# Input projection of a hybrid attention layer: each 128-row matmul issued as two 64-row matmuls, one on each half of the array

## What is computed

```
h = rms_norm(x) * norm_pre
p = h @ w_in                       # 2048 -> 7168 columns: q, k, v, gate of heads A (12), B (12 q / 4 kv), C (8)
oa = stick_breaking(qa, ka, va)    # causal over everything before
ob = band_attention(qb, kb, vb, 2 chunks back, alibi, sinks)
oc = band_attention(qc, kc, vc, 8 chunks back, relative bias)
o = concat(oa * silu(ga), ob * silu(gb), oc * silu(gc)) @ w_out
y = x + rms_norm(o) * norm_post    # and the new k, v rows as outputs
```

## Time and profile before

| | |
|---|---|
| median of three executions | 1939.62 us |
| span of the profiled execution, first to last instruction | 1936.8 us |
| PE busy | 1905.3 us, 98% |
| DVE busy | 1240.0 us, 64% |
| ACT busy | 666.4 us, 34% |
| share of PE in the chain that ended last | 86%, of it 61 points products |
| mean granted clock of TensorE | 0.997 |
| DMA | 301 MB, mean 155 GB/s |

### The profile page before, as it was taken

The page is one execution under the profiler, slowest core; times in us unless marked ns, Lnnn a source line. Parts: engine busy times, 40 slices in busy tenths (PEclk is TensorE's granted clock), DMA queues, the critical chain, the costliest instruction groups (busy, mean ns, idle before and its releaser), DMA issues.

```text
span 1936.8 us, 30940 instructions
## 1 busy us (share of the span) xinstructions
PE 1905.3 (98%) x12508; PEld 1746.7 (90%) x12508; DVE 1240.0 (64%) x2224; ACT 666.4 (34%) x1257; POOL 53.3 (3%) x119
## 2 busy tenths in 40 slices
PE   6999999999999999999999999999999999999997
PEld 5999999999999999999999999999999988888886
DVE  7358777787878778553544454355525566766878
ACT  7124233343433334222222222233213354344453
POOL 4000000000000000000000000000000000000131
PEclk9999999999999999999999999999999999999999
DMA  6456777676777767666657667465446657555396
GB/s 245 117 120 137 159 157 165 145 147 154 146 162 154 162 146 149 151 137 136 149 119 155 141 136 143 104 141 123 106 97 144 136 197 278 192 175 187 121 258 226
DMA packets 880407, 301.05 MB, mean 155 GB/s; under 512 B 618504, under 2 KB 845592, under 8 KB 878968
## 3 DMA queue, kind: packets, MB, share of 16 engines
q1 hardware_dynamic: 877192, 290.35, 61.6%
q0 software_dynamic: 3072, 8.73, 2.2%
HBM read 210.45 MB, written 96.20 MB: 158 GB/s over the span
## 4 chain that ended last, share of the span: by engine, by line
PE 86%; DVE 9%; DMA 1%; ACT 1%; issue 1%; POOL 0%; SPq 0%; DVEq 0%; ACTq 0%; POOLq 0%
PE ps L1204 21%; PE ps L1205 20%; PE ps L1206 20%; PE ps L1400 4%; PE ps L1401 4%; PE ps L1402 4%; PE ps L1292 3%; PE ps L1371 3%; PE ps L1264 2%; PE ps L1342 2%; DVE arena L1853 1%; DVE act_lo L1740 1%; DVE arena L1733 1%; DMA b_out<-in_w_out_dram 1%; DVE arena L1841 1%
## 5 line engine op out<-in xcount | busy, mean ns | idle before, releaser
L1204 PE MATMUL ps<-act_hi,w_hi 128*128 128x352 f32 x2688 | 878.8, 327 | 0.1
L1206 PE MATMUL ps<-act_hi,w_lo 128*128 128x352 f32 x2688 | 863.7, 321 | 0.0
L1205 PE MATMUL ps<-act_lo,w_hi 128*128 128x352 f32 x2688 | 863.6, 321 | 0.0
L1204 PEld LDWEIGHTS ps<-act_hi,w_hi 128*128 128x128 f32 x2688 | 505.2, 188 | 24.7 <-issue 20.7
L1205 PEld LDWEIGHTS ps<-act_lo,w_hi 128*128 128x128 f32 x2688 | 506.1, 188 | 0.0
L1206 PEld LDWEIGHTS ps<-act_hi,w_lo 128*128 128x128 f32 x2688 | 504.9, 188 | 0.0
L1501 ACT ACTIVATE w_hi<-w_raw 128x512 fp32r<-128x512 f32 x224 | 139.3, 623 | 340.5 <-DMA w_raw<-in_w_in_dram 340.4
L1748 DVE TENSOR_TENSOR w_lo<-w_raw,w_hi 128x512 fp32r<-128x512 f32 x224 | 150.9, 675 | 51.5 <-ACT w_hi L1501 51.2
L1568 ACT ACTIVATE arena<-arena,small 128x257 f32<-128x257 f32 (+6 forms) x180 | 101.3, 565 | 209.1 <-DVE small L1891 209.1
L2079 DVE STREAM_TRANSPOSE arena<-arena 128x1024 f32<-128x1024 f32 (+4 forms) x100 | 132.6, 1326 | 40.0 <-ACT arena L1691 39.2
L1691 ACT ACTIVATE arena<-arena 128x1024 f32<-128x1024 f32 (+1 forms) x60 | 61.0, 1017 | 255.8 <-DVE arena L1865 255.7
(11 more groups left out here) (182 smaller groups left out, 2105.5 us busy)
## 6 DMA issues: line engine op xcount, KB each, us to landing
w_raw<-in_w_in_dram SPq DMA_DIRECT2D x176, 256.0 KB, 3.3
weight_scratch<-arena SPq DMA_DIRECT2D x216, 128.0 KB, 3.4
arena<-weight_scratch SPq DMA_DIRECT2D x54, 512.0 KB, 4.5
b_out<-in_w_out_dram SPq DMA_DIRECT2D x72, 256.0 KB, 3.3
w_raw<-in_w_out_dram SPq DMA_DIRECT2D x70, 256.0 KB, 2.7
w_raw<-in_w_in_dram SPq DMA_DIRECT2D x96, 128.0 KB, 3.1
weight_scratch<-arena SPq DMA_DIRECT2D x80, 132.0 KB, 4.1
arena<-weight_scratch SPq DMA_DIRECT2D x40, 256.0 KB, 3.3
```

What stands on the lines that cost most here:

```text
L1204: mm(bank(g, GN), wh, ah, start=(k == 0), stop=False)
L1205: mm(bank(g, GN), wh, al, start=False, stop=False)
L1206: last = mm(bank(g, GN), wl, ah, start=False, stop=(k == KT - 1))
```

## The change

Tiles 1 to 55 get another way of being multiplied; tile 0 keeps `product`. Each 128-row matmul becomes two of 64 rows, one on partitions 0 to 63 (`upper`), one on partitions 64 to 127 (`lower`), with the same 128 output partitions and 352 columns. Both add into the same PSUM bank, but not at the same time: in the list of PE an upper matmul number x is followed by the lower matmul number x - 15, which belongs to another group and so to another bank. The first lower matmul of a product waits until its upper twelve are done, the first upper one of the next quarter until the lower twelve are done. A tick now holds 12 upper and 12 lower matmuls, and a product is complete 15 matmuls (1.25 ticks) later than before. For that, all attention is moved back by one tick (`SLOT`), the fetching and splitting of weights too (`piece_at`), and the evacuation of a group by 1.2 ticks. The counts of the semaphore `piece_used` are adapted, since each product now adds to it.

```diff
-SLOT = [12 * (FIRST[u] - 1) for u in range(NU)]
+SLOT = [12 * (FIRST[u] - 1) + 1 for u in range(NU)]
...
+LAG = 15
+def used_no(T, q, g=2):
+    return 9 * T + (3 * g + q if T == 0 else 3 * q + g) + 1
...
 def piece_at(T, q):
-    return 12 * (T - 2) + 3 * q + 3.0
+    return 12 * (T - 2) + 3 * q + 4.0
...
-    plan += [(12 * (T - 1) + 9.9 + g, "out", T, g) for T in range(TILES) for g in range(GROUPS)]
+    plan += [(12 * (T - 1) + 11.1 + g, "out", T, g) for T in range(TILES) for g in range(GROUPS)]
...
-            def project(T, n):
-                q, g = divmod(n, GROUPS)
-                if g == 0:
-                    pe.wait_ge(lo_made, 4 * T + q + 1)
-                if q == 0:
-                    pe.wait_ge(proj_out, 3 * (T - 1) + g + 1)
-                last = product(g, q)
-                if q == 3:
-                    last.then_inc(proj_done, 1)
-                elif g == GROUPS - 1:
-                    last.then_inc(piece_used, 1)
+            def half_product(half, n, x):
+                q, g = divmod(n, GROUPS)
+                kk, part = divmod(x, 3)
+                k, hp = 4 * q + kk, slice(64 * half, 64 * half + 64)
+                w = (w_hi, w_hi, w_lo)[part][hp, q, P * kk:P * kk + P]
+                a = (act_hi, act_lo, act_hi)[part][hp, k, GN * g:GN * g + GN]
+                return mm(bank(g, GN), w, a, start=(half == 0 and k == 0 and part == 0),
+                          stop=(half == 1 and k == KT - 1 and part == 2), skip_group_check=True)
+            def upper(s, x):
+                T, n = s // 12 + 1, s % 12
+                q, g = divmod(n, GROUPS)
+                if x == 0:
+                    if g == 0:
+                        pe.wait_ge(lo_made, 4 * T + q + 1)
+                    if q == 0:
+                        pe.wait_ge(proj_out, 3 * (T - 1) + g + 1)
+                    else:
+                        pe.wait_ge(piece_used, used_no(T, q - 1, g))
+                last = half_product(0, n, x)
+                if x == 11:
+                    last.then_inc(upper_done, 1)
+            def lower(s, x):
+                T, n = s // 12 + 1, s % 12
+                if x == 0:
+                    pe.wait_ge(upper_done, s + 1)
+                last = half_product(1, n, x)
+                if x == 11:
+                    last.then_inc(proj_done if n >= 9 else piece_used, 1)
+            def project(s):
+                for x in range(12 * s, 12 * s + 12):
+                    upper(s, x % 12)
+                    if x >= LAG:
+                        lower((x - LAG) // 12, (x - LAG) % 12)
+                if s + 1 == TICKS:
+                    for x in range(12 * TICKS - LAG, 12 * TICKS):
+                        lower(x // 12, x % 12)
```

More of the change, by code:

```diff
@@ L468, in sp_plan @@
             k, v = 12 * TILE_OF["k", u], 12 * TILE_OF["v", u]
-            plan += [(k + 3.0, "store_keys", u, 0), (v + 0.6, "part_values", u, 0), (v + 8.0, "load_values", u, 0),
+            plan += [(k + 3.0, "store_keys", u, 0), (v + 1.6, "part_values", u, 0), (v + 8.0, "load_values", u, 0),
                      (v + 12.0, "store_values", u, 0), (cache_at(u), "cache_keys", u, 0), (SLOT[u] + (14.5 if 0 < u < NA else 10.5 if u == NA else 6.0), "cache_values", u, 0)]
@@ L768, in build @@
         hi_made, lo_made, piece_used = sem("hi_made"), sem("lo_made"), sem("piece_used")
-        proj_done, proj_out = sem("proj_done"), sem("proj_out")
+        proj_done, proj_out, upper_done = sem("proj_done"), sem("proj_out"), sem("upper_done")
         kc_in, kc_turned, vc_in = sem("kc_in"), sem("kc_turned"), sem("vc_in")
@@ L918, in in_piece @@
                 if T and q < 3:
-                    sp.wait_ge(piece_used, 3 * (T - 1) + q + 1)
+                    sp.wait_ge(piece_used, used_no(T - 1, q))
                 elif T:
@@ L1064, in piece_out @@
                 elif r < 3:
-                    sp.wait_ge(piece_used, 3 * (TILES - 1) + r + 1)
+                    sp.wait_ge(piece_used, used_no(TILES - 1, r))
                 else:
@@ L1085, in mixed_load @@
                 if q < 3:
-                    sp.wait_ge(piece_used, 3 * (TILES - 1) + q + 1)
+                    sp.wait_ge(piece_used, used_no(TILES - 1, q))
                 else:
@@ L1225, in first_project @@
                     last = product(g, q)
[L1226 to L1229, removed]
+                    last.then_inc(proj_done if q == 3 else piece_used, 1)
             def set_ready(key):
@@ L1427, in _ @@
                 if what == "product":
-                    project(u, n)
+                    project(12 * (u - 1) + n)
                 elif what == "scores" and UNITS[u][0] == "a":
@@ L1589, in left_high @@
                 else:
-                    act.wait_ge(piece_used, 3 * (TILES - 1) + (1, 1, 2, 2, 2, 2, 3, 3)[k])
+                    act.wait_ge(piece_used, used_no(TILES - 1, (0, 0, 1, 1, 1, 1, 2, 2)[k]))
                 wait_left_raw(act, i, k)
@@ L1600, in sample_high @@
                     return
-                act.wait_ge(piece_used, 3 * TILES)
+                act.wait_ge(piece_used, 9 * TILES)
                 if n == 2:
```

## The result

The changed kernel takes **1972.47 us** (median of four executions, 1969.58 to 1973.47), the kernel before 1939.25 us in the same job (four, 1938.63 to 1939.85). The ratio is 1.017 with an interval of 1.0157 to 1.0184: 33 us slower, where 65 us faster had been forecast. The profiled execution of the changed kernel took 1972.42 us; its span is 1970.7 us, 33.9 more than before.

A forecast was written before the change was run, and what follows sets the result against it. PE was taken to bound the kernel, busy for 1905 of 1937 us. The terms, -63.4 - 14.0 + 2.3 + 10 = -65.1 us, gave 1874.5 us, with a range of 1846 to 1948.

The forecast's parts named there:

- term 1: Product matmuls: a pair of 64-row halves leaves a 4.3 ns gap beyond streaming instead of 12.3 ns; -63.4 us.
- term 4: Evacuation of product groups from PSUM: PE waits where DVE is late, one wait a tile; +10 us, 16.6 at most.
- Rival (a): Product matmuls: the 12.3 ns gap stays for each half; 1936 us, 1928 without waits, 1945 with all; chance 0.36.
- Term 2: Between scores and products: 70 changes of the array's form, 0.20 us each, are spared; -14.0 us.
- Term 3: Start and end of the products: fifteen upper and fifteen lower halves run without a partner, 15 slots more; +2.3 us.
- At nothing: Weight fetch and split, semaphore waits of lower matmuls, and PE's issue of two loads and two matmuls: no cost.
- Rival (b): Product pairs: float32r weight loads of the halves go one after the other, 212 to 217 ns; some 2370 us; chance 0.14.
- (c): Product pairs: each costs 1 to 3 ns more than a whole matmul, +16 us; about 1952 us; chance 0.08.

## Why the prediction was wrong

Two steps failed: the gap that term 1 took from the scores, which had to bring nearly all of the gain, and the size of the waits in term 4.

- **Term 1** (-63.4 us) failed and gave 0. The step in question was "I take 4.3 ns, a pair every 151 ns, since the scores are the nearest rows in form". The gap is the same for a whole matmul, a pair and a lone half: 159.1 ns each. What makes the scores' gap small is not their 64 rows. The prediction named the row that said so, the float32 passes on all 128 rows with 0.43 to 0.46 us for 0.427, and made it a rival. They are float32 like the scores, with a load for each pass, but stand on all 128 rows (and on 64 output partitions): a small gap does not need the 64 rows. The pass of 0.43 us and a pair at the lower clock both take 0.83 to 0.84 ns a column, and both show next to no gap; whether the type or the pace decides, no run separates. Rival (a), with a chance of 0.36, had the size by symmetry: each half gets what the whole array got.
- **Term 2** (-14.0) was right in the main: 0.20 us at the place shown, -12.6 us between the two kernels with ACT's evacuation, -10.7 in the change itself, where waits lie in the same steps. The page "TensorEngine Tiling (Array Packing)" of the Trainium skill (Key Properties) says that a change of tiling mode drains TensorE; the trace agrees and gives the price, 0.09 us to drain and 0.11 for the load behind.
- **Term 3** (+2.3) was right: the 30 lone halves have the ordinary step, 15 x 0.159 = 2.4.
- **Term 4** (+10, at most 16.6) was too small: 32.9 us. The mechanism was named, and for the v tiles the size was near (11.6 us of idle time), though there the due times are enough and the later product is not needed (9.9 with whole matmuls). The bound was wrong in three ways. It took the evacuations of k tiles to keep their place, though the list of DVE has one a unit behind four scans now; this was half of it (16.0 us). It counted only one wait a tile. And it counted no cost but the idle time, where a wait also costs the overlap with the last pair and uncovers a load. The clock behind waits, 6.4 us, stood in no term.
- **Sum by the same terms with the measured values**: 0 - 10.7 + 31.4 + 5.8 + 4.8 + 2.1 = +33.4. Rival (a)'s highest time, 1945, used the same bound of 16.6 and was 27 us short, so the range, which took (a) as its far end, did not hold. The rows of one v tile gave no bound for what happens at the k tiles.
- **At nothing**: right. The issue of four records in 159 ns holds (halves and whole have the same step), no wait of the products for the splitting stands in PE's view of waits. The queue that loads instructions moved 2.64 MB instead of 1.62, with no stop of PE to be seen for it.
- Rival (b) is refuted by every pair: the loads overlap. So is (c), 159.1 against 159.1.

What stays open: what the gap is, of which a bfloat16 step keeps 8.7 ns; why the clock falls behind some waits of 2 us and not behind others; and one to two us of ordinary steps in the kernels with halves.

## What to carry over

Splitting a full-height matmul into row halves bought no throughput here: the gap is as long for a half, a pair and a whole matmul, and the halves only pay where they spare a change of the array's form, 0.20 us each. A change that lets results come later by a tick must be checked in the list of the engine that takes them out, entry by entry, since two tenths of a tick decided between ahead of and behind a 2.4 us block; a wait there costs 0.28 us more than its idle time, and sometimes the clock. The slack of an idle engine (ACT here, 15.5 us) was worth more than the order on the busy one.

## What the hardware showed beyond this

- A 64-row float32r matmul alone, a pair on the two halves, and a whole one: 159.1 ns a step each for 352 columns at 2.4 GHz. At 1.2 GHz nine steps of pairs take 287.14 - 284.50 = 2.64 us, 293 ns each, and 352 columns at that rate are 293 ns: there is no gap.
- With only the upper half of the array in use, the granted clock is 0.93 in a stretch in which PE is busy for 98%, and 0.98 over 300 us without a pause of PE.
- In runs of twelve only three matmuls at each border find the other half free in time; the kernel takes 619 us more than the one before.
- bfloat16 takes 3.7 ns off a float32r matmul of 352 columns, no more. The Trainium skill ("TensorE: Matmul & The Clock Gate", The mechanism, on packed matmuls) says of loads under a matmul in flight both that they overlap only where the rows differ and that a load into the array's background buffer is pulled ahead. The trace goes against the first taken alone: a load of all 128 rows, 188 ns long, belongs to every 128-row matmul, and the step is 159.1 ns, shorter than the load. A load that is not hidden costs 0.11 us more, as behind the wait shown.
